# Prompt attention of a hybrid decoder step on one core: the last two index heads of each key chunk go from VectorE to GpSimd

## The reference

```python
def indexer_select(qi, wi, kidx, q_pos, k_sel):
    L = kidx.shape[1]
    s = jnp.einsum('bqhd,bsd->bqhs', qi, kidx)
    s = jnp.einsum('bqhs,bqh->bqs', jax.nn.relu(s), wi).astype(jnp.float32)
    ...
    _, sel = lax.top_k(s, k_sel)
    return sel
```

## Time and profile before

| | us |
|---|---|
| median of 3 runs | 2982.63 (2981.66 to 2983.72) |
| the profiled execution | 2981.48, its span 2979.7 |
| PE busy | 2708.7 (91%) |
| DVE busy | 1923.7 (65%) |
| ACT busy | 816.9 (27%) |
| POOL busy | 39.0 (1%) |

### The profile page before, as it was taken

How to read it: one execution, slowest core, us unless ns; L and a number is a source line. 1 busy time by engine, 2 the same in 40 slices (tenths; PEclk the granted TensorE clock), 3 DMA queues, 4 the chain that set the end, 5 groups by cost and what they waited for, 6 DMA issues and landing times. The chain is left out here.

```text
span 2979.7 us, 30785 instructions
## 1 busy us (share of the span) xinstructions
PE 2708.7 (91%) x11266; PEld 1414.1 (47%) x11266; DVE 1923.7 (65%) x3904; ACT 816.9 (27%) x1382; POOL 39.0 (1%) x48
## 2 busy tenths in 40 slices
PE   7987999999999999999999987999999659889896
PEld 5643444454454544545454544455555424334344
DVE  4209899979797898979899982159961032424422
ACT  4212233222323323232424233122204420220201
POOL 0000000000000000000000000000000000000000
PEclk9998999999999999999999998999999879899996
DMA  7111111111111110111010101412246484323116
GB/s 208 28 29 39 43 40 40 40 42 39 39 38 33 39 43 28 39 32 44 25 44 25 35 22 30 144 60 100 97 118 196 170 264 189 141 106 134 50 36 18
DMA packets 196833, 215.19 MB, mean 72 GB/s; under 512 B 81360, under 2 KB 162896, under 8 KB 193040
## 3 DMA queue, kind: packets, MB, share of 16 engines
q1 hardware_dynamic: 192000, 161.75, 18.9%
q0 software_dynamic: 4688, 51.53, 5.2%
HBM read 157.53 MB, written 55.72 MB: 72 GB/s over the span
## 5 line engine op out<-in xcount | busy, mean ns | idle before, releaser
L783 PE MATMUL attn_ps_r<-xnT,attn_w_rest 128*128 128x424 f32 (+2 forms) x2464 | 993.3, 543 | 30.6 <-ACT attn_rest L634 15.7
L115 DVE TENSOR_SCALAR_CACHE_REDUCE attn_hits<-attn_acc,attn_search 128x384 uint8<-128x384 f32 (+13 forms) x448 | 662.0, 1478 | 11.5
L783 PEld LDWEIGHTS attn_ps_r<-xnT,attn_w_rest 128*128 128x128 f32 x2464 | 443.1, 191 | 441.6 <-issue 424.1
L1094 PE MATMUL samp_ps_r<-xnT,samp_w_rest 128*128 128x424 f32 (+1 forms) x800 | 291.1, 527 | 19.9 <-DMA samp_w_rest<-in_w_in 13.3
L653 ACT ACTIVATE attn_probT<-attn_ps_p 128x512 f32<-128x512 f32 (+1 forms) x288 | 151.7, 571 | 405.4 <-PE attn_ps_p L828 405.3
L1622 PE MATMUL merge_ps_y<-merge_w_out,merge_merged 128*128 128x512 f32 (+1 forms) x544 | 235.3, 594 | 0.0
L1094 PEld LDWEIGHTS samp_ps_r<-xnT,samp_w_rest 128*128 128x128 f32 x800 | 154.5, 194 | 154.3 <-issue 132.9
L1610 PE MATMUL merge_ps_u<-merge_attn,merge_up_a 128*128 128x512 f32 (+1 forms) x320 | 138.2, 604 | 84.5 <-DVE merge_attn L1654 81.0
L711 DVE SCALAR_TENSOR_TENSOR attn_acc<-attn_relu,iw,attn_acc 128x512 f32<-128x512 f32 (+3 forms) x266 | 182.1, 684 | 30.9 <-ACT attn_relu L670 3.0
L813 PE MATMUL attn_ps_s<-kT,qT 64*128 64x512 f32 (+3 forms) x640 | 162.9, 588 | 26.0 <-DVE attn_chunk_max L740 18.9
L634 ACT ACTIVATE attn_rest<-attn_ps_r 128x424 f32<-128x424 f32 (+1 forms) x130 | 67.8, 522 | 427.3 <-PE attn_ps_r L783 425.9
(11 more groups left out here) (225 smaller groups left out, 2259.6 us busy)
## 6 DMA issues: line engine op xcount, KB each, us to landing
attn_w_rest<-in_w_in SPq DMA_DIRECT2D x100, 256.0 KB, 3.4
rest_t<-attn_rest SPq DMA_DIRECT2D x104, 212.0 KB, 2.0
merge_gates<-rest_t SPq DMA_DIRECT2D x8, 2048.0 KB, 12.0
rest_t<-samp_rest SPq DMA_DIRECT2D x40, 212.0 KB, 2.0
norm_x_in<-in_x_prompt SPq DMA_DIRECT2D x16, 512.0 KB, 4.0
merge_x<-in_x_prompt SPq DMA_DIRECT2D x4, 2048.0 KB, 8.1
out_y_prompt<-merge_y SPq DMA_DIRECT2D x16, 512.0 KB, 2.6
rest_t<-attn_rest SPq DMA_DIRECT2D x26, 208.0 KB, 2.1
```

Of the source, the lines that this page charges most:

```text
L115: self.v.done(self.nc.vector.tensor_scalar(self.hits, self.x, limit, None, op, ALU.add, accum_out=self.count))
L783: ins = nc.tensor.matmul(ps_r[:, 0:width], w_rest[:, n % 2, k, :], c.xnT[:, k, t0:t0 + width], start=(k == 0), stop=(k == KC - 1))
L1094: ins = nc.tensor.matmul(ps_r[:, i % 2, 0:width], w_rest[:, j % 2, k, :], c.xnT[:, k, t0:t0 + width], start=(k == 0), stop=(k == KC - 1))
```

## The change

Heads 6 and 7 of each chunk, the last pair, are no longer added by DVE. POOL, which so far was idle in this stage, waits for their relu, multiplies each in place in `relu` by its weight, waits for both, and adds the second to the first. DVE adds this sum to `acc` with one plain addition (`add_last`). Where a further chunk follows in the tile, this addition stands in DVE's order behind the first two sums of that chunk; after the last chunk it stands directly behind head 5. `summed` now counts 7 per chunk, and `sums(pair)` tells ACT what count frees a pair's half of `relu`: for the last pair of a chunk it is the count behind that addition. The plan of PE's work is the same.

```diff
+        self.sums0 = before([7 * len(x) for x in self.idx])
...
+    def sums(self, pair):
+        T = max(T for T in range(len(self.pairs0) - 1) if self.pairs0[T] <= pair)
+        ch, n = divmod(pair - self.pairs0[T], 4)
+        first = self.sums0[T] + (7 * ch - 1 if ch else 0)
+        if n < 3:
+            return first + 2 * (n + 1) + (1 if ch and n else 0)
+        return self.sums(pair + 1) + 1 if ch + 1 < len(self.idx[T]) else self.sums0[T + 1]
...
+            @block.gpsimd
+            def _(pool):
+                for T in range(NT + 2):
+                    for ch, (_, width) in enumerate(plan.idx[T]):
+                        pair = plan.pairs0[T] + ch * 4 + 3
+                        parts = [relu[:, pair % 2, hh, 0:width] for hh in range(2)]
+                        pool.wait_ge(rectified, pair + 1)
+                        for hh in range(2):
+                            h = NI - 2 + hh
+                            nc.gpsimd.tensor_scalar(parts[hh], parts[hh], c.iw[:, T * NI + h:T * NI + h + 1], None,
+                                                    ALU.mult).then_inc(scaled, 1)
+                        pool.wait_ge(scaled, 2 * (pair // 4 + 1))
+                        nc.gpsimd.tensor_tensor(parts[0], parts[0], parts[1], ALU.add).then_inc(paired, 1)
...
                             act.wait_ge(scored, pair + 1)
                             if pair >= 2:
-                                act.wait_ge(summed, 2 * (pair - 1))
+                                act.wait_ge(summed, plan.sums(pair - 2))
...
+                def add_last(T, ch):
+                    pair, (k0, width) = plan.pairs0[T] + ch * 4 + 3, plan.idx[T][ch]
+                    dve.wait_ge(paired, pair // 4 + 1)
+                    dve.wait_ge(summed, plan.sums(pair) - 1)
+                    nc.vector.tensor_tensor(acc[:, k0:k0 + width], acc[:, k0:k0 + width], relu[:, pair % 2, 0, 0:width],
+                                            ALU.add).then_inc(summed, 1)
...
-                        for h in range(NI):
+                        for h in range(NI - 2):
...
                             if h:
-                                dve.wait_ge(summed, 2 * plan.pairs0[T] + ch * NI + h)
+                                dve.wait_ge(summed, plan.sums(pair) - 2 + h % 2)
...
                             ins.then_inc(summed, 1)
+                            if ch and h == 1:
+                                add_last(T, ch - 1)
+                    if plan.idx[T]:
+                        add_last(T, len(plan.idx[T]) - 1)
```

More of the change, by code:

```diff
@@ L534, in stage_prompt_attention @@
         ps_r = m.psum("ps_r", [P, 512])
-        (scored, rectified, summed, multiplied, biased, maxed, exped, turned, turned_kept, weighted, inverted,
+        (scored, rectified, scaled, paired, summed, multiplied, biased, maxed, exped, turned, turned_kept, weighted, inverted,
          normalised, stored, rest_done, rest_kept, own, w_in0, w_in1, rest_stored0, rest_stored1) = [m.sem(n) for n in (
-            "scored", "rectified", "summed", "multiplied", "biased", "maxed", "exped", "turned", "turned_kept",
+            "scored", "rectified", "scaled", "paired", "summed", "multiplied", "biased", "maxed", "exped", "turned", "turned_kept",
             "weighted", "inverted", "normalised", "stored", "rest_done", "rest_kept", "own",
@@ L699, in _ @@
                     for ch, (k0, width) in enumerate(plan.idx[T]):
-                        out = acc[:, k0:k0 + width]
-                        for h in range(NI):
+                        for h in range(NI - 2):
                             pair = plan.pairs0[T] + ch * 4 + h // 2
+                            out = acc[:, k0:k0 + width]
                             iw = c.iw[:, T * NI + h:T * NI + h + 1]
@@ L719, in _ @@
                     if now:
-                        dve.wait_ge(summed, 2 * plan.pairs0[T + 1])
+                        dve.wait_ge(summed, plan.sums0[T + 1])
                         v.done(nc.vector.tensor_tensor(acc[:, LB:L], acc[:, LB:L], later[:], ALU.add))
```

## The result

The changed kernel takes 3087.2 us (median of 4 runs, 3085.5 to 3093.5) against 2982.1 (2980.4 to 2983.7) for the kernel before on the same chip: a ratio of 1.0356, 95% interval 1.0338 to 1.0374. The forecast was slower by 53 us, 3036 us with a range up to 3068; it is slower by 105, and the time lies above the range. The profiled execution has a span of 3084.8 us against 2979.7: 105.1 us more.

A forecast was written before the change was run, and what follows sets the result against it. PE was 91% busy, DVE with little to spare. 31 us for full chunks, 18 for narrow ones and 4 for ends make 53 on 2981.48: 3034.5, as median 3036 us; own range 3020 to 3053, wider range 2998 to 3068.

The forecast's parts named there:

- The held buffer: Between chunks: buffer 1 stays taken until DVE adds POOL's sum behind the next chunk's first two sums, at 3.88 us.
- the two exposed relus: Per further chunk: DVE idles for the relus before heads 0 and 2, 2.3 us with handovers against 0.92 saved.
- the period: Time per full chunk followed by another: 7.77 us without turns, 8.97 with them, against 6.88 on average before.
- POOL's scaling: POOL's weighting of one head at 512 columns: 0.63 us assumed, between 0.55 and 1.13.
- the select's price plus that: Price of a 512-column scaling: 128-column select 0.282 us plus a write's 0.344 for 384 columns more, 0.63.
- the point of decision: End of the next chunk's heads 0 and 1, at 3.09 us; a shorter POOL chain does not alter the period.
- rival 2: POOL at upper prices, chain 4.7 us: period 9.4 without turns (3051 us) or 11.0 with them (3093); chance 0.18.
- turns: POOL and DVE in SBUF alternate by whole instructions, adding 1.2 us to each full chunk's period.
- the absorption at the phase's end: Late ends, about 1.2 us on average, vanish in DVE's waits at tile starts, counting only in tiles 2, 4, 5, 6: 4 us.
- 15 x (8.97 - 6.88): Loss over 15 full chunks followed by another, new period less the old mean: 31 us.

The follow-up runs named there:

- third experiment: POOL takes heads 6 and 7 in each tile's last chunk only, the other 24 chunks staying as in the kernel before: 3013.0 us, ratio 1.0103.
- the order alone: Changed kernel with POOL clearing one column in place of its two scalings and addition: 3005.6 us against 2984.1 for the kernel before.

## Why the prediction was wrong

**The direction and the mechanism held.** The held buffer, the two exposed relus and the period were as worked out: 7.75 us against 7.77 with POOL at no cost. The relu of the second pair is released by the new addition. The rest of the tiles kept its length to 2.5 us in sum.

**The term that was mis-sized is POOL's scaling.** 0.63 us was put together from a write and a 128-column select; the bounds were 0.55 and 1.13. Within the changed kernel these two stand one after the other, at a phase's end in tile 15, the first beside DVE's last sum, the second and the addition with DVE idle:

```profile
1738.39 1.92 POOL L640 TENSOR_SCALAR attn_relu<-attn_relu,iw 128x512 f32<-128x512 f32 x1 [4.70 <-ACT attn_relu L697]
1740.30 1.56 POOL L640 TENSOR_SCALAR attn_relu<-attn_relu,iw 128x512 f32<-128x512 f32 x1
1741.94 1.27 POOL L643 TENSOR_TENSOR attn_relu<-attn_relu 128x512 f32<-128x512 f32 x1
```

So it is 1.56 us alone and 1.92 beside DVE. The select of 128 columns was no price for it: a scaling of 128 columns takes 0.64 on average and 0.60 alone, so the 384 columns more take 0.96 us, where the write's take 0.344. The step that failed is "I take the select's price plus that": it lets arithmetic cost per column what a write costs. And four times 0.282 was no bound either, since it prices another instruction. With the chain at 4.9 us and the point of decision at 3.09, it was rival 2's mechanism that ran, through its dear scaling and not through its dear addition: 9.6 us for a period against the 9.4 it gave without turns.

**The second wrong step is the absorption at the phase's end.** "A shift of 1.2 us in the tile ahead of such a wait is absorbed" counted 4 of 17 us. The third experiment shows 31 us of ends and a kernel 29 us slower. DVE's waits for the relu before a first sum were not drawn on, since between the late end and such a wait PE itself waits for DVE's maxima.

**The third is what the period was set against.** "15 x (8.97 - 6.88)" takes a mean that counts first gaps, which PE fills and the hold leaves alone. Tile 15 shows the right base: its phase is 13.05 us longer (38.89 - 25.84), of which 3.3 are its end (third experiment); the 9.7 left are three holds of 3.23, and 9.62 - 6.39 is 3.23. For 15 chunks the difference of base is 7 us at most.

**The account.** 104 us of phases are 31 of ends (third experiment) and, by subtraction, 73 in the 24 chunks behind them, 3.0 each. The prediction had 4 and 49. Of the 51 us missed 27 lie in the ends: 13 are the absorption (17 to 4), 14 the price of POOL's chain. 24 lie in the periods: 7 are the base, and the other 17 are what is left of two errors that run against each other, POOL's chain sized too small and the turns too large (29 of the 49 were turns). Without that luck the forecast would have been further off. Rival 2's sum without turns, with the measured period, base and ends, is 15 x 3.23 + 9 x 2.4 + 31 = 101 of the 104. By another cut: the order alone 22, POOL's addition 10, its two scalings 74.

**Turns.** The prediction had every pair of instructions that meet take turns, and 1.2 us of it in each period. The rule holds for POOL's addition, but the meeting seldom comes. In the changed kernel DVE's sums average 0.786 us, 0.035 more than before: of 140 only 4 start under POOL's addition, and 6 are held by a scaling. POOL's first scaling is longer by 0.36 where it starts beside DVE's last sum. In the period of 9.62 us that is the smaller part; the scalings alone, at their lone price, are 3.1 of POOL's 4.9. Two places where a DVE instruction starts second, in tiles 8 and 15:

```profile
702.60 1.27 POOL L643 TENSOR_TENSOR attn_relu<-attn_relu 128x512 f32<-128x512 f32 x1
702.61 1.54 DVE L745 TENSOR_SCALAR attn_acc<-attn_relu,iw 128x512 f32<-128x512 f32 x1 [3.07 <-ACT attn_relu L697]
...
1722.04 1.37 POOL L643 TENSOR_TENSOR attn_relu<-attn_relu 128x512 f32<-128x512 f32 x1
1722.39 1.56 DVE L747 SCALAR_TENSOR_TENSOR attn_acc<-attn_relu,iw,attn_acc 128x512 f32<-128x512 f32 x1
```

The first sum (0.48 us alone) takes 1.54 and ends 0.28 behind POOL's addition, the other (0.75 alone) 1.56 and ends 0.54 behind it. In the period shown with the result it is the other way round: the sum starts at 1712.23, POOL's addition at 1712.78, and the sum takes its 0.75.

**What stays open.** Why a POOL scaling takes longer than a two-tensor multiply of the same size was not tried beyond the constant. Nor is it explained why a scaling holds DVE's sum for less than its own length, where POOL's two-tensor instructions hold it to their end. What the 24 inner chunks cost with two buffers is a difference of two runs: no run has POOL in them alone with two.

## What to carry to other kernels

An engine that takes work over also takes over its buffer: before counting what the relieved engine saves, follow who gives the buffer back, when, and who stands behind it in order. Price the moved instruction on its new engine by the same instruction there; if the trace has none, no other instruction is an upper bound, and the range has to be wide. Set a new period against the chunks that it will lengthen, not against a mean over all of them. A delay at a phase's end need not be absorbed by the waits of the next phase: here a third engine in between waited too, and 31 us of late ends made 29 us of time.

## What the runs showed of the hardware

- On POOL a scaling of 128 x 512 f32 in place takes 1.56 us alone with its factor by pointer and 1.49 with a constant (means of 1.73 and 1.64, in part beside DVE); the same product as an operation on two tensors takes 1.04 alone (mean 1.21), an addition 1.27.
- POOL's reads stretch DVE's sums with two tensor inputs, its writes don't (0.751 us beside them, as with POOL idle); the one-input DVE scaling is stretched by writes (0.48 to 0.69).
- Who starts first is served first: a DVE sum that starts under a POOL instruction on two tensors is held until that one is through (0.55 us behind its end, up to 1.57 in place of 0.75), and one that starts before it keeps its 0.75.
- DVE starts 0.03 us behind POOL's end when it waits for it (1714.10 to 1714.13), so the hand-over itself costs next to nothing there.
